# HGRN stage: memory heads between the input units, gate last, ladder steps between the last units

## The reference, cut to what matters

```python
h = x @ a_w_in[layer]
q, f_raw, i_in, g, qm = jnp.split(h, [768, 1536, 2304, 3072], axis=-1)
logf = jnp.logaddexp(log(lb), log1p(-lb) + log_sigmoid(f_raw)); kh = -jnp.expm1(logf)
# S_t = diag(f_t) S_{t-1} + k_t^T v_t ;  o_t = q_t S_t      (q = silu(q) * 128**-0.5, v = i_in)
o = gla_chunkwise(q, kh, i_in, logf)
o = o * rsqrt(mean(o**2) + eps) * gnorm * silu(g)
mem_out = softmax(qm @ mem_k.T / 8) @ mem_v
x = post_norm(x, concat([o, mem_out]) @ w_o[layer], ...)       # then the mixture of experts
```

## Time and profile before

| | us |
|---|---|
| median of 3 runs | 1509.99 |
| lowest, highest | 1509.79, 1515.02 |
| the profiled execution | 1512.15 |
| its span in the profile | 1510.5 |
| PE busy in the span | 1380.8 (91%) |
| DVE busy | 1044.0 (69%) |
| ACT busy | 763.4 (51%) |

### The profile page before, as it was taken

How to read it: one execution, slowest core, us unless ns; L and a number is a source line. 1 busy time by engine, 2 the same in 40 slices (tenths; PEclk the granted TensorE clock), 3 DMA queues, 4 the chain that set the end, 5 groups by cost and what they waited for, 6 DMA issues and landing times.

```text
span 1510.5 us, 19563 instructions
## 1 busy us (share of the span) xinstructions
PE 1380.8 (91%) x7482; PEld 1178.0 (78%) x7482; DVE 1044.0 (69%) x1068; ACT 763.4 (51%) x745; POOL 85.8 (6%) x80
## 2 busy tenths in 40 slices
PE   5996999999899999999997788999988978999995
PEld 5975778887799778887997677788878967788884
DVE  7685668887676574545436758888885365788886
ACT  2665344344433434343445135677764484577773
POOL 0010000100000000000000010300003000400000
PEclk9998999999999999999998898999998999799998
DMA  9984559997575376555455022999993711399991
GB/s 361 384 295 142 171 200 304 298 311 266 186 252 167 112 243 195 178 192 167 140 167 174 23 59 69 305 328 346 350 314 104 238 52 57 112 321 345 346 356 52
DMA packets 205901, 327.72 MB, mean 217 GB/s; under 512 B 9520, under 2 KB 140272, under 8 KB 205824
## 3 DMA queue, kind: packets, MB, share of 16 engines
q1 hardware_dynamic: 192528, 276.71, 54.3%
q0 software_dynamic: 13296, 49.93, 9.9%
HBM read 325.56 MB, written 1.05 MB: 216 GB/s over the span
## 4 chain that ended last, share of the span: by engine, by line
PE 73%; DVE 15%; ACT 7%; issue 3%; DMA 1%; SPq 0%; POOL 0%; DVEq 0%; ACTq 0%; POOLq 0%
PE ps L2023 21%; PE ps L2025 21%; PE ps L2024 21%; DVE w_low L1249 4%; ACT w_high L650 3%; PE ps L2534 1%; PE ps L2628 1%; PE ps L2303 1%; PE ps L2203 1%; DMA raw<-in_w_qkv 1%; DVE stats L1754 1%; DVE h_low L1908 1%; PE ps L2216 1%; DVE scratch L1682 1%; DVE x_rows L1745 1%
## 5 line engine op out<-in xcount | busy, mean ns | idle before, releaser
L1249 DVE TENSOR_TENSOR w_low<-raw,w_high 128x2048 fp32r<-128x2048 f32 (+1 forms) x256 | 588.2, 2303 | 295.8 <-ACT w_high L650 293.8
L650 ACT ACTIVATE w_high<-raw 128x2048 fp32r<-128x2048 f32 (+1 forms) x256 | 484.1, 1894 | 365.0 <-PE ps L2025 337.6
L2023 PE MATMUL ps<-w_high,h_high 128*128 128x512 f32 (+1 forms) x896 | 354.7, 396 | 11.4 <-DVE h_low L1342 4.0
L2025 PE MATMUL ps<-w_high,h_low 128*128 128x512 f32 (+1 forms) x896 | 348.4, 389 | 0.0
L2024 PE MATMUL ps<-w_low,h_high 128*128 128x512 f32 (+1 forms) x896 | 348.3, 389 | 0.0
L2023 PEld LDWEIGHTS ps<-w_high,h_high 128*128 128x128 f32 x896 | 170.1, 190 | 46.4 <-issue 7.2
L2025 PEld LDWEIGHTS ps<-w_high,h_low 128*128 128x128 f32 x896 | 169.8, 189 | 35.1
L2024 PEld LDWEIGHTS ps<-w_low,h_high 128*128 128x128 f32 x896 | 170.0, 190 | 32.6 <-issue 0.2
L2023 PE MATMUL ps<-h_high,w_high 128*128 128x256 f32 x592 | 172.6, 292 | 11.9 <-DVE h_low L1342 6.3
L2024 PE MATMUL ps<-h_low,w_high 128*128 128x256 f32 x592 | 171.0, 289 | 0.0
L2025 PE MATMUL ps<-h_high,w_low 128*128 128x256 f32 x592 | 170.9, 289 | 0.0
(11 more groups left out here) (335 smaller groups left out, 1481.2 us busy)
## 6 DMA issues: line engine op xcount, KB each, us to landing
raw<-in_w_down SPq DMA_DIRECT2D x124, 512.0 KB, 5.1
raw<-in_w_gate_up SPq DMA_DIRECT2D x88, 512.0 KB, 5.1
scratch<-in_w_ada POOLq DMA_DIRECT2D x40, 1024.0 KB, 5.6
raw<-in_w_gate SPq DMA_DIRECT2D x80, 512.0 KB, 5.2
raw<-in_w_up SPq DMA_DIRECT2D x80, 512.0 KB, 6.6
raw<-in_w_qkv SPq DMA_DIRECT2D x24, 512.0 KB, 12.7
raw<-in_w_o SPq DMA_DIRECT2D x24, 512.0 KB, 6.3
raw<-in_w_in SPq DMA_DIRECT2D x24, 512.0 KB, 4.9
```

What stands on the lines that cost most here:

```text
L650: act.activation(wh[u % SPL][:, :, 0:w], raw[u % RAW][:, :, 0:w], ACT.Copy).then_inc(h_split, 1)
L1249: dve.tensor_tensor(wl[u % SPL][:, :, 0:w], raw[u % RAW][:, :, 0:w], wh[u % SPL][:, :, 0:w].bitcast(F32), ALU.subtract).then_inc(l_split, 1)
L2023: pe.matmul(o, h1, h2, start=start, stop=False, skip_group_check=True)
L2025: return pe.matmul(o, l1, h2, start=False, stop=stop, skip_group_check=True)
```

## The change

The columns of the input product come in another order: chunk 0 is qm and the first 256 of f, chunk 1 the rest of f, chunk 2 the first 512 of q, chunk 3 ("mixed") the rest of q and the last 256 of i, chunk 4 the first 512 of i, chunks 5 and 6 are g, and its last 256 columns are now the narrow units u12 and u13. A new helper on SP loads a unit from two places, with rows of 256 columns.

PE does the memory scores between u2 and u3, the transposes between u4 and u5 and after u5, the memory outputs after u6 and after u7. The ladder begins after u8: step (0,0), then half of u9, step (0,1), the other half, and from there one step and one gate block of 128 columns in turn (12 blocks: u10 to u13). Steps (7,0) to (8,1) have no block behind them. The score banks are always 4 to 7, one pair for each half.

On DVE the memory steps, the decays and the ladder are put among the splits; `SPLITS_IN` places the splits of u12, u13, u14 and u15 behind the ladder steps (3,0), (4,0), (5,1) and (7,0). The levels 6 to 8 are no longer copied by DVE under a mask but by ACT (`late_take`): block by block from a band of partitions, 2 instructions for each half of level 6, one for levels 7 and 8. DVE no longer scales q by 128**-0.5; ACT adds its logarithm as a bias in the exponential that makes the keys. The zeroing of `scD` moves from DVE to POOL, to just before the stage. The two `h_low` of the memory heads become one. The low part of u16 and its high part, which were made before the memory heads, now stand behind the ladder.

The diff, cut to its core (helpers that only repeat a moved loop are left out):

```diff
-            for c0, w in ((0, 512), (512, 512), (1024, 512), (1536, 512), (2048, 256), (2304, 512), (2816, 512)):
-                columns(A["a_w_in_2"][0], c0, w)
+            for c0, c1 in ((4 * MIX, MIX), (MIX + FW, None), (0, None), (NC, 2 * MIX + NC), (2 * MIX, None), (3 * MIX, None)):
...
+            columns(A["a_w_in_2"][0], 3 * MIX + NC, FW)
...
+            pool.memset(scD, 0.0).then_inc(scores_cleared, 1)
...
+                if l < 8:
+                    m = 2 ** (l - 1)
+                    for b in range(0, P, 2 * m):
+                        i = act.activation(
+                            scD[b:b + m, hs, :].rearrange("p h (c t) -> p (h c) t", c=2)[:, :, b + m:b + 2 * m],
+                            ps[b:b + m, o:o + 2, :].rearrange("p a (b t) -> p (a b) t", t=P)[:, 0:HG, b + m:b + 2 * m], ACT.Copy)
...
+            exps(MEM[0], MEM_BANKS, 0)
+            exps(MEM[0], MEM_BANKS, 1)
...
+            ahead(PLAN["a_in"] + 13)
+            for u in range(2):
+                late_take(6, u)
+            for u in range(2):
+                late_take(7, u)
+            done(6)
+            features(16, 2, ACT.Silu)
...
+            for u in range(2):
+                late_take(8, u)
+            act.preload_act_table_set("natural_log_exp_and_others")
             ahead(PLAN["wo1"])
-            act.preload_act_table_set("natural_log_exp_and_others")
-            heads(MEM[0], LATE_BANKS)
...
+            SPLITS_IN = {(3, 0): 10, (4, 0): 11, (5, 1): 12, (7, 0): 13}
+            for l in range(8):
...
+                    if l < 6:
+                        take(l, u)
+                    if (l, u) in SPLITS_IN:
+                        ahead(PLAN["a_in"] + SPLITS_IN[l, u])
...
+            chunk("features", fresh=True)
+            chunk("features", between=lambda: mem_scores(0, 15))
+            chunk("features", between=lambda: mem_turns(0, 0))
+            mem_turns(0, 1)
+            mixed_chunk(2, lambda w: mem_outs(0, w))
...
+                    piece = 2 * l + u
+                    if piece < 2:
+                        half_rows(ps[:, piece, :], UK, piece, False, True)
+                        lin[0] += piece
+                    elif piece < 14:
+                        gate_block(piece - 2)
```

More of the change, by code:

```diff
@@ new lines, in _ @@
+            act.activation(kd, kd, ACT.Exp).then_inc(act_step, 1)
+            act.wait_ge(act_step, step.up())
+            act.activation(kd, kd, ACT.Ln, bias=1.0).then_inc(exp_ready, 1)
+            act.wait_ge(exp_ready, exr.up())
+            mem_turn_out(0, 0)
+            ahead(PLAN["a_in"] + 5)
+            act.wait_ge(qk_in, dkr.up())
+            act.activation(FT[:, 6:12, :], sfx, ACT.Exp, bias=st[:, 64:65], scale=-1.0).then_inc(exp_ready, 1)
+            act.wait_ge(exp_ready, exr.up())
@@ new lines, in _ @@
+            lin[0] += 1
+            ahead(PLAN["a_in"] + 7)
+            head_out(mem_out(0), FT[:, 18:19, :])
+            done(3)
+            features(4, 2, ACT.Silu, last=False)
+            act.activation(tv[:, :, 512:768], pair(1, 2).rearrange("p a (t n) -> p (a t) n", t=TT), ACT.Copy).then_inc(lin_evac, 1)
+            act.wait_ge(lin_evac, evac.up())
+            lin[0] += 1
+            head_out(mem_out(1), FT[:, 19:20, :])
+            ahead(PLAN["a_in"] + 9)
+            done(4)
+            rows(0, 512)
@@ L2230, in heads, with mem_scores @@
                 er.n += 2
+            def mem_scores(l, evacuated):
+                pe.wait_ge(lin_evac, evacuated)
+                for w in range(2):
+                    for a, m in enumerate(MEM[l][w]["heads"]):
+                        for c0, c1, x, y in m["scores"]:
+                            i = pe.matmul(ps[:, 4 + 2 * w + a, c0:c1], x, y, start=True, stop=True, skip_group_check=True)
+                    i.then_inc(s_ready, 1)
+                    sr.up()
+                er.up(2)
@@ new lines, in mem_turns, with mem_outs @@
+            def mem_turns(l, w):
+                pe.wait_ge(p_ready, pr.up())
+                for a in range(2):
+                    for x, y in MEM[l][w]["turns"]:
+                        i = pe.transpose(ps[:, 4 + 2 * w + a, y:y + P], prob(w)[:, a, x:x + P], ident[:, :])
+                i.then_inc(pt_ready, 1)
+                ptr.up()
+            def mem_outs(l, w):
+                pe.wait_ge(pt_evac, pte.up())
+                for a, m in enumerate(MEM[l][w]["heads"]):
+                    for q, (t0, t1, val, c0) in enumerate(m["outs"]):
+                        i = pe.matmul(ps[64 * a:64 * a + 64, 4 + 2 * w, t0:t1], val, turned(w, MEM[l][w])[:, a, c0:c0 + t1 - t0],
+                                      start=q == 0, stop=q == 1, skip_group_check=True)
+                i.then_inc(o_ready, 1)
+                orr.up()
@@ new lines, in half_rows @@
+            def half_rows(bank, k0, t, first, last):
+                if t == 0:
+                    pe.wait_ge(l_split, lsp.up())
+                u, tok = n[0] % SPL, slice(t * P, (t + 1) * P)
+                for k in range(UK):
+                    i = mm3(bank, hh[:, k0 + k, tok], hl[:, k0 + k, tok], wh[u][:, k, :], wl[u][:, k, :],
+                            first and k == 0, last and k == UK - 1)
+                if t:
+                    i.then_inc(unit_used, 1)
+                    used.up()
+                    n[0] += 1
```

239 lines of the change are left out of this document (152 added, 87 removed).

## The result

| | before | after |
|---|---|---|
| median of the runs | 1511.34 (4 runs) | 1489.12 (4 runs) |
| lowest, highest | 1509.79, 1515.02 | 1486.99, 1490.94 |
| ratio | | 0.9848 [0.983, 0.9866] |
| the profiled execution | 1512.15 | 1486.99 |
| its span | 1510.5 | 1485.3 |

The kernel became faster by 22.2 us by these medians, by 25.2 by the two profiled executions. The forecast was 1484.4, in a range of 1482 to 1492. A second measurement of both kernels gave 1511.87 and 1488.04, so 23.8 us.

The account below looks back on a forecast made before the run. PE, busy nine tenths of the span, bounds the kernel, so only its waits can be won. Units 74.4, memory heads 6.1 and ladder 19.3 end at 840.4, squares at 851.7: 25.6 us off 1509.99 gives 1484.4, range 1482 to 1492.

Parts of the forecast that it names:

- The base: Starting time the 25.6 us were taken from: median of three, 1509.99; from the profiled execution, 1512.15, it gave 1486.5.
- The units and the cover of the memory heads: Input units take PE 74.4 us; memory heads between them cost only 6.1, their waits hidden.
- The slow rival: From first memory score to last block, small groups hold PE at 1.2 GHz: 60 us more, 1544; chance 0.04.
- The pause: PE's wait at u10 behind a table load and two exponentials: 4.3 us, plus 2.5 of low clock, both go.
- The ladder: Steps (0,0) to (6,1) between unit blocks: 19.3 us on PE, 2.82 per step and block, DVE hidden.
- The late copies: ACT's copies of levels 6 to 8: 0.33 us for 192 columns, 0.49 for 384; only (8,1)'s on the path.
- The end of the ladder: Behind (6,1), without cover: DVE products, (8,1), copy, table load 1.28, split 1.91; squares at 851.7 instead of 877.3.
- The clock at the end: Rival: PE's clock falls behind pauses of 2 to 3 us after the ladder; 22.6 gained, 1487.4; chance 0.28.
- No overlap: Rival: ladder steps wait for DVE, 12 steps of up to 1.8 us, 21 us lost: 1505.5; chance 0.05.
- everything from there on moves as one: From u14 on, all shifts with the first h_low, 7.7 us after the squares begin; u17 waits for the same loads.

Follow-up runs that it names:

- e1_again: The changed kernel timed once more, unaltered; median 1488.04, ratio 0.9832 to the kernel before.
- e11: The changed kernel with the memory heads' scores, turns and outputs as one block behind u3, not between the units; 1493.18, ratio 0.9867.
- e5_apart: The changed kernel with the ladder behind all units and gate blocks, low parts of u12 to u15 made before it; 1492.34, ratio 0.9865.
- e7: The kernel before, with ACT's split of u10 put ahead of the table load and two exponentials; 1513.15, ratio 1.0004.
- e3: The changed kernel with the ladder's end rearranged: table load between the level 8 copies, u16's split behind the last h_high and h_low; 1485.38, ratio 0.9825.
- e9_tail3: The kernel of e3 with the split of u17 ahead of the router's weights on ACT, its low part likewise on DVE; 1481.81, ratio 0.9801.
- e6_dvecopy: The changed kernel with the copies of levels 6 to 8 back on DVE instead of ACT; 1487.55, ratio 0.9838.
- e8_tail: The changed kernel with only ACT's end rearranged: table load behind the last silu, u16's split between the level 8 copies; 1486.49, ratio 0.9825.

## Why the prediction was right, point by point

**The base.** The forecast set 25.6 us against a median of three, 1509.99. Over the 48 executions of the kernel before that stand beside the runs here the median is 1512.57, over the 9 of the changed kernel 1488.51: a gain of 24.1. Of the 4.7 us between 1484.4 and 1489.12 the larger half is this base: the prediction had the profiled execution (1512.15) in hand as well. That 1486.5 from it came within 0.5 of the profiled execution after is partly luck: 1.7 us won ahead of the stage and 1.7 lost in the experts cancel, and the profiled execution of e1_again, the same kernel, took 1491.28. The 25.9 us of the stage for 25.6 are not luck of that kind, since the stage came out the same in both profiles of the changed kernel.

**The units and the cover of the memory heads**: right. No pause, clock 1.00, and e11 puts a price on the cover, 7.4 us. The slow rival did not come: 357 records stand at 1.00 from 798 to 842. The Trainium skill ("TensorE: Matmul & The Clock Gate", A second HAM failure mode: psum-queue depth-cycling) puts the swinging clock down to PE being idle for short times between such groups. The ladder of the changed kernel is no test of that, since PE is never idle in it. The ladders with pauses are, and they don't agree: before, with 13 waits of up to 0.9 us, and e5_apart, with 10 of up to 1.1 us, the clock is 1.00 from 849 to 875 and from 825 to 852.

**The pause**: its length and its going were right. As a price for one cause it was wrong: e7 shows that 4.3 + 2.5 us could not have been had by moving one split ahead of what the prediction named. In the new order the pause is gone; which part of the order is needed for that no run shows.

**The ladder**: 2.82 us a step forecast, 2.77 measured; DVE hidden, with 0.57 to spare in each step of level 1.

**The late copies**: 0.33 and 0.49 forecast; 0.66 for two of 192 columns, 0.47 to 0.49 for 384. Nearest rows of the same engine, scaled by columns, were good to 0.02.

**The end of the ladder**: the scores of (7,0), the products for (7,1) and the squares were forecast at 842.1, 846.8 and 851.7, which is 101.5, 106.2 and 111.1 from the first matmul of u0. Measured, from that matmul at 738.9: DVE takes up the scores of (7,0) at 839.87 and is done with the products for (7,1) at 844.41, the squares start at 849.73, so 100.9, 105.5 and 110.8. So the forecast was 0.7 too late up to the products and 0.4 too early from there to the squares, where the low clock in (8,1) lies (below); the two hide each other in part. Table load and split stand on the path with 1.28 and 1.91, as forecast. The row of the load ends at 847.90 and the split starts at 847.91. The Trainium skill's drain of 1380 ns on top ("ScalarE: Activation LUTs", What ACT_TABLE_LOAD costs) is not to be seen in this place either; it would have put the squares at 851.1. The low part of u16 ahead of the scaling was to make DVE start 1.7 us late and cost nothing: DVE starts 2.4 us behind the squares for 0.7 before, and the first `h_low` comes 7.1 us behind them for 7.0.

**The clock at the end**: the rival happened, at a smaller price than the 3 us of the forecast. The clock did fall behind both pauses, 0.83 from 842 to 852 and 0.92 in u14 to u17. The first fall cost 0.6 at the squares, by (8,1), which is 1.55 for 0.94 and stands between the products for (7,1) and ACT's last copy. It cost no more because the outputs of the heads, slow as well, lay beside ACT's table load and split: two heads were ready at 848.4, before ACT came at 849.7. The second cost 0.6 against the kernel before. So each fall cost what of its slow stretch lay on the chain, not its length.

**No overlap**: the price of this rival is 1484.4 + 21, so 1505.4 and not 1505.5, and 12 x 1.8 is 21.6; neither changes its place in the forecast.

**What "everything from there on moves as one" left out**: the split of u17 behind the router's loads. In the changed kernel it cost nothing, so the forecast was not hurt; but it was the next bound, 4.6 us as soon as the squares came earlier (e3), and the prediction, which named the wait of u17 for those loads, did not lay it against PE's time.

**What stays open**: of the 25.9 us, the runs put 4.7 on the interleaved ladder and 7.4 on the cover of the memory heads. Each was priced with the other in place, so that they may be added is taken for granted, not shown. The remaining 13.8 are, by the rows, the pause with its low clock (6.8) and the waits around the old memory block (7.5 by e11's block), 14.3 together; this is a sum of rows, no run separated them.

## What to carry to other kernels

Where PE is busy for nine tenths, look for the stretches where it is not and ask what independent work could stand beside the waiting chain; here putting the attention's small pieces between weight units won more than the interleaved recurrence. A pause that comes out of two engines' fixed orders doesn't go when one instruction is moved: lay out both queues up to the next two units before pricing it. And when a chain is made shorter, look at once at what its engines have queued behind a wait for a load: one split put ahead of such a wait turned a gain of 0.3 us, from the start of the stage to the post-norm, into 5.8 (e3_tail2, e9_tail3).

## What the runs showed of the hardware

The same pause did not always have the same effect on the clock. Ahead of u14 PE pauses 2.19 us in the changed kernel, in e5_apart and in e11_heads_alone, and has been busy for 5.08 us of the 7.1 from squares to first `h_low` in the first two. In the changed kernel the stretch of u14 to u17 then has a clock of 0.92 (above), and so it has in e1_again. In e5_apart, the first matmul of u14 and the busy time of the same stretch:

```profile
867.41 0.47 PE L2105 MATMUL ps<-w_high,h_high 128*128 128x512 f32 x1 [2.19 <-DVE h_low L1801]
```
```profile
866.60:887.30 20.70, 19.65 (x85) 15.92 (x86) 7.57 (x8) 8.94 (x9) 5.56 (x9) 1.00 0.36 93
```

There it is 1.00. So behind the same pause of 2.2 us the stretch is 1.1 us longer in one kernel than in the other (21.8 for 20.7); what decides it the runs don't show. It is not the fall at the end of the ladder alone: in e11_heads_alone the clock is 0.72 in the six microseconds ahead of the squares, as in the changed kernel, and 1.00 in u14 to u17. Pauses of 1.79 (before, e6_dvecopy, e7_earlysplit, e8_tail, e9_tail3) left the clock of that stretch at 1.00; one of 5.89 (e11_heads_alone) was followed by 0.50 from 770 to 775.
